# Moving the further block to the seventh pair, w3 of the last pair in three loads, and another order of the last sums and of the last norm

## The chip, the core and the metric

The kernel runs on one core of a Trainium2 chip. The metric is the device time of one execution in microseconds; the median of three runs of the kernel before is 714.94 us (714.26 to 716.94). A core has five engines that run side by side and meet only at semaphores: TensorE (PE in the rows; PEld is its weight load), VectorE (DVE), ScalarE (ACT), GpSimd (POOL) and SyncE (SP), which here issues nearly all DMA transfers.

## What is computed

One layer of an encoder: 512 tokens of width 1024 go through a mixer and then through a mixture of 32 experts with a normed output. The mixer takes the first third of the time and is not touched. Cut to the part that the change touches, the reference is:

```python
# h: the normed tokens (512 x 1024); two experts are chosen for each token
hid = jax.nn.silu(xb @ w1[e]) * (xb @ w3[e])      # w1, w3: 1024 x 512, for each expert e
y   = (hid @ w2[e]) * wt[:, None]                 # w2: 512 x 1024
out = out.at[row_tok].add(y)                      # back to the tokens
x   = x + g2 * out
return rms_norm(x) * final_g
```

All is float32. The weights of the 32 experts are 192 MB, read once.

## The kernel before

**Pairs.** The experts are worked through two at a time, in 16 pairs (`pair(p)`, p = 0 to 15; the last is `LAST`). Each expert has 64 places for tokens (`CAP`), so a pair fills the 128 partitions. For a pair TensorE multiplies with w1 (`up_product(n0, xg, 0)`, line L1002), then adds up four groups of the pair before (`combine_before`, L1024 and L1025: two products for each of the eight groups of 128 tokens by 512 columns), multiplies with w3 (L1002 again), adds up the other four groups, turns the hidden rows (L971), turns the rows gathered for the next pair (L963), and multiplies with w2 in two halves of 512 columns (`down_half`, L1016). VectorE weighs each half with the router's weight (`weighted`, L1895), ScalarE makes its high part (L1514), VectorE its low part (`low_part`, L1900); these feed the sums of the next pair. VectorE adds each finished group to the tokens (L1905).

**Weights.** The six matrices of a pair are six units of 2 MB. Unit n goes to slot n modulo 9 (eight slots of `ring` and one of `mid`). SyncE loads the units in order (`expert_unit`, L518) and waits before each for the slot to be used up (`slot_used_up`), so one held slot holds back every load behind it. The loads of the last pair are cut in pieces (`last_pair_units`, L570): w1 and w3 in halves, w2 as its first 512 columns and two quarters of the others; `up_product` and `down_half` wait for the pieces one by one.

**The further block.** An expert with more than 64 tokens needs further blocks of 64; here there is one. The expert of the first of them is swapped to place `XPLACE` = 2 `XPAIR`, so that its weights come with pair `XPAIR`, and the block is worked beside that pair: its slots are made in pair `XBEGIN` = `XPAIR` - 3, its rows are turned in `XTURN` = `XPAIR` - 1 (L1033), its products run in `XPAIR` (L1046 with w1 and w3, L1061 with w2), and its sums in the two pairs behind (L1071). The three units that it uses (`HELD`) are free only after L1046 or L1061. Behind pair `LATER` = `XPAIR` + 2 every engine asks whether there are more blocks. `XPAIR` is 9.

**The end.** Behind the last w2 product TensorE adds up the eight groups of the last pair, first the four of the low 512 columns (`HALVES_FIRST`), then the four others. VectorE adds them (`last_add`). ScalarE squares each group into a sum (L1550) and takes the root for each of the four token tiles (L1565); VectorE takes the reciprocal (L2077) and scales the high half of each tile (L2079). GpSimd multiplies the low halves with `final_g` (L2167, into `gained`), and ScalarE scales them (L1555). SyncE stores a tile when both its halves are done (L602).

## Time and profile before

| | us |
|---|---|
| median of 3 runs | 714.94 (714.26 to 716.94) |
| the profiled execution, its own time | 715.57 |
| its span, first to last instruction | 712.8 |
| TensorE busy | 672.9 (94%) |
| VectorE / ScalarE / GpSimd busy | 344.5 / 177.5 / 61.6 |
| bytes moved by DMA | 253.19 MB |
| mean granted TensorE clock | 0.992 |

All times in rows are microseconds from the start of the span, unless marked ns. A row of the timeline gives start, duration, engine, line, operation and tile; "x32" means that 32 like instructions were merged. In brackets stands how long the engine was idle before, and who released it. The chain is the work that ended last, followed back from the last instruction.

### The profile page before, as it was taken

The page shows a single profiled execution, that of the slowest core. Times are in us where ns is not written, and L with a number is a line of the kernel's source. Part 1 is how long each engine was busy: PE and PEld are TensorE (multiplying, and loading weights), DVE is VectorE, ACT ScalarE, POOL GpSimd, SP SyncE. Part 2 cuts the span into 40 slices and gives each one's busy share as a digit, 9 for nine tenths or more (in the row PEclk, how much of TensorE's full clock was granted, in tenths as well). Part 3 has the DMA queues.
Part 4 walks back from the last instruction along what each step waited for, and adds up shares of the span by engine and source line. Part 5 has one row for each costly group of instructions (what it writes and reads, how often), then busy time and mean ns, then how long its engine had stood idle before and what let it go on. Part 6 is the DMA issues. An engine that isn't in the chain of part 4 may idle for free.

```text
span 712.8 us, 9269 instructions
## 1 busy us (share of the span) xinstructions
PE 672.9 (94%) x3703; PEld 364.6 (51%) x3703; DVE 344.5 (48%) x648; ACT 177.5 (25%) x322; POOL 61.6 (9%) x59
## 2 busy tenths in 40 slices
PE   2999999999999899999999998898999999999993
PEld 2676787866878434344344343443344343443441
DVE  3546988798977723333334332332144433332336
ACT  4333468323424211110110110101021110111115
POOL 2017900100000100000000000000000000000003
PEclk9999999999999999999999999999999999999997
DMA  9998355666369599999999999999999999999982
GB/s 330 388 375 315 118 189 195 241 235 235 117 238 354 226 419 431 424 425 428 426 425 427 427 427 424 417 425 426 428 426 428 426 425 428 425 425 425 417 332 118
DMA packets 41595, 253.19 MB, mean 355 GB/s; under 512 B 4304, under 2 KB 4688, under 8 KB 28496
## 3 DMA queue, kind: packets, MB, share of 16 engines
q1 hardware_dynamic: 37008, 243.82, 83.8%
q0 software_dynamic: 2624, 4.74, 1.8%
q10 hardware_dynamic: 1920, 4.04, 1.5%
q8 instruction: 30, 0.49, 0.3%
q14 instruction: 13, 0.11, 0.0%
HBM read 252.84 MB, written 4.19 MB: 361 GB/s over the span
## 4 chain that ended last, share of the span: by engine, by line
PE 78%; DMA 15%; ACT 3%; DVE 3%; issue 1%; ACTq 0%; SPq 0%; POOLq 0%; DVEq 0%
PE bank L1002 26%; PE bank L692 18%; DMA ring<-in_w 13%; PE bank L1016 13%; PE bank L1024 3%; PE bank L1025 3%; PE bank L963 2%; PE bank L639 1%; PE bank L816 1%; PE bank L1046 1%; PE bank L971 1%; PE bank L656 1%; PE bank L794 1%; PE bank L804 1%; DMA xg_rows<-x_rows,keep 1%
## 5 line engine op out<-in xcount | busy, mean ns | idle before, releaser
L1002 PE MATMUL bank<-ring,low 128*64 128x512 f32 x944 | 228.8, 598 | 9.9 <-DMA ring<-in_w 8.7
L1002 PEld LDWEIGHTS bank<-ring,low 128*64 128x64 f32 x944 | 75.2, 138 | 130.3 <-issue 129.4
L1905 DVE TENSOR_TENSOR x<-x,bank 128x512 f32<-128x512 f32 x136 | 84.5, 681 | 80.9 <-PE bank L1025 80.9
L1016 PE MATMUL bank<-ring,low 128*64 128x512 f32 x432 | 114.0, 596 | 0.3 <-ACT low L1502 0.3
L1016 PEld LDWEIGHTS bank<-ring,low 128*64 128x64 f32 x432 | 35.0, 137 | 64.8 <-issue 63.0
L1895 DVE SCALAR_TENSOR_TENSOR y_raw<-bank,keep,g2b 128x512 f32<-128x512 f32 x32 | 24.0, 750 | 86.7 <-PE bank L1016 86.7
L2021 DVE TENSOR_TENSOR low<-low,bank 128x512 f32<-128x512 f32 x16 | 11.0, 688 | 97.8 <-PE bank L1002 97.8
L1024 PE MATMUL bank<-y_hi,slot_tok 128*128 128x512 f32 x128 | 53.7, 419 | 0.2 <-DVE y_lo L1900 0.2
L1502 ACT COPY low<-bank 128x512 f32<-128x512 f32 x16 | 9.4, 586 | 165.7 <-PE bank L971 165.7
L1025 PE MATMUL bank<-y_lo,slot_tok 128*128 128x512 f32 x128 | 50.4, 393 | 0.0
L2133 POOL DMA_INDIRECT xg_rows<-x_rows,keep x16 | 16.0, 999 | 372.7 <-PE bank L963 288.4
L1514 ACT CAST y_hi<-y_raw 128x512 fp32r<-128x512 f32 x32 | 19.8, 618 | 106.5 <-DVE y_raw L1895 106.5
L692 PE MATMUL bank<-h_hi,w_hi 128*128 128x512 f32 x96 | 38.4, 400 | 1.1 <-DVE h_lo L1614 1.1
L1024 PEld LDWEIGHTS bank<-y_hi,slot_tok 128*128 128x128 f32 x128 | 24.0, 187 | 29.1 <-issue 24.3
L692 PE MATMUL bank<-h_lo,w_hi 128*128 128x512 f32 x96 | 37.4, 390 | 0.0
L692 PE MATMUL bank<-h_hi,w_lo 128*128 128x512 f32 x96 | 37.4, 390 | 0.0
L1002 PE MATMUL bank<-mid,low 128*64 128x512 f32 x80 | 35.4, 595 | 0.7 <-DMA ring<-in_w 0.7
L1016 PE MATMUL bank<-mid,low 128*64 128x512 f32 x80 | 35.6, 596 | 0.0
L1609 DVE TENSOR_TENSOR w_lo<-ring,w_hi 128x512 fp32r<-128x512 f32 x32 | 25.0, 785 | 20.4 <-ACT w_hi L1299 20.2
L1496 ACT ACTIVATE low<-bank 128x512 f32<-128x512 f32 x16 | 9.6, 599 | 99.6 <-PE bank L1002 99.6
L1900 DVE TENSOR_TENSOR y_lo<-y_raw,y_hi 128x512 fp32r<-128x512 f32 x32 | 22.1, 692 | 21.3 <-ACT y_hi L1514 21.2
L1299 ACT CAST w_hi<-ring 128x512 fp32r<-128x512 f32 x32 | 19.7, 617 | 39.5 <-PE bank L692 34.2
(279 smaller groups left out, 890.2 us busy)
## 6 DMA issues: line engine op xcount, KB each, us to landing
ring<-in_w SPq DMA_DIRECT2D x76, 2048.0 KB, 27.1
ring<-in_w_mod SPq DMA_DIRECT2D x11, 2048.0 KB, 11.7
mid<-in_w SPq DMA_DIRECT2D x10, 2048.0 KB, 28.7
ring<-in_w SPq DMA_DIRECT2D x18, 1024.0 KB, 24.7
ring<-in_w_in SPq DMA_DIRECT2D x3, 2048.0 KB, 22.5
ring<-in_w_out SPq DMA_DIRECT2D x2, 2048.0 KB, 11.0
x<-in_x SPq DMA_DIRECT2D x4, 512.0 KB, 5.5
ring<-in_w_in SPq DMA_DIRECT2D x2, 1024.0 KB, 18.7
```

Of the source, the lines that this page charges most:

```text
L692: last = mm(out_, lhs, rhs, start=k == 0 and n == 0, stop=stop and n == 2)
L1002: last = mm(bk[e * CAP:(e + 1) * CAP, :], xb[:, k, e * CAP:(e + 1) * CAP], unit(n % SLOTS, KD)[:, k, :], start=k == 0, stop=k == KD - 1)
L1016: last = mm(bk[e * CAP:(e + 1) * CAP, :], hid_t[:, k, e * CAP:(e + 1) * CAP], unit(n % SLOTS, KF)[:, k, hf * 512:(hf + 1) * 512], start=k ...
L1024: mm(bk[:, :], slot_tok[:, buf, t * P:(t + 1) * P], hi[:, c], start=True, stop=False)
L1025: return mm(bk[:, :], slot_tok[:, buf, t * P:(t + 1) * P], lo[:, c], start=False, stop=True)
L1299: nc.scalar.copy(w_hi[:, c % DEPTH, :], raw_chunk(c)).then_inc(w_hi_ready, 1)
L1514: nc.scalar.copy(y_hi[:, c], y_raw[:, c]).then_inc(yh_ready, 1)
L1609: v.tensor_tensor(lo, raw_chunk(c), hi.bitcast(F32), ALU.subtract).then_inc(w_lo_ready, 1)
L1895: return v.scalar_tensor_tensor(raw[:, c], (Y0, Y1)[hf][:, :], w_slot[:, buf:buf + 1], g2b[:, c], ALU.mult, ALU.mult)
L1900: return v.tensor_tensor(lo[:, c], raw[:, c], hi[:, c].bitcast(F32), ALU.subtract)
L1905: return v.tensor_tensor(acc[:, t, c], acc[:, t, c], bk[:, :], ALU.add)
L2133: return g_.indirect_dma_start(rows_[:, :], None, x1_row, bass.IndirectOffsetOnAxis(ap=row_of[:, buf:buf + 1], axis=0), bounds_check=S - 1 ...
```

## The change

Four things are changed. `XPAIR` goes from 9 to 6, and with it the place of the swapped expert and every step of the further block. The w3 units of the last pair are loaded in three pieces (half, quarter, quarter) in place of two halves; `up_product` waits for the pieces with a new semaphore `third_in`. In the last pair the first four sums stand ahead of the last quarter of the w2 product, and with them VectorE's first four adds and ScalarE's first four squares stand ahead of the second half's low and high parts. In the last norm GpSimd scales the low halves of tiles 0 and 1, and ScalarE those of tiles 2 and 3, behind all its squares and roots.

```diff
-XPAIR = 9
+XPAIR = 6
...
             def last_pair_units(k):
-                pieces = (((slice(0, kk // 2), slice(0, 512)), (slice(kk // 2, kk), slice(0, 512))) if k < 4 else
-                          ((slice(0, kk), slice(0, 512)), (slice(0, kk // 2), slice(512, D)),
-                           (slice(kk // 2, kk), slice(512, D))))
+                pieces = (((slice(0, 4), slice(0, 512)), (slice(4, KD), slice(0, 512))),
+                          ((slice(0, 4), slice(0, 512)), (slice(4, 6), slice(0, 512)), (slice(6, KD), slice(0, 512))),
+                          ((slice(0, KF), slice(0, 512)), (slice(0, 2), slice(512, D)), (slice(2, KF), slice(512, D))))[k // 2]
+                second_in = third_in if k < 4 else middle_in
...
-                sp.wait_ge(fin_low, t + 1)
+                if t < 2:
+                    sp.wait_ge(fin_low_pool, t + 1)
+                else:
+                    sp.wait_ge(fin_low, t - 1)
...
-                        if k == KD // 2 and n0 == FIRST[LAST]:
-                            pe.wait_ge(landed[n % SLOTS], landed_at(n))
+                        if n0 == FIRST[LAST]:
+                            if k == 4 and w == 1:
+                                pe.wait_ge(third_in[e], 16)
+                            elif k == (4, 6)[w]:
+                                pe.wait_ge(landed[n % SLOTS], landed_at(n))
...
+            def last_sums(hf):
+                pe.wait_ge(yl_ready, 2 * LAST + 1 + hf)
+                for i in range(4 * hf, 4 * hf + 4):
+                    combine_group(HALVES_FIRST[i], LAST % BUFS, y_hi, y_lo, EXTRA_BANKS[i]).then_inc(c_done, 1)
...
+                if p == LAST:
+                    down_half(n0, 0).then_inc(y_done, 1)
+                    down_half(n0, 1, 0, KF // 2)
+                    pe.wait_ge(pt_ready, PAIRS)
+                    pe.wait_ge(acc_done, 8 * LAST)
+                    last_sums(0)
+                    down_half(n0, 1, KF // 2, KF).then_inc(y_done, 1)
+                    last_sums(1)
+                    return
...
             for t in range(NT):
                 halfs_square(t, 1, ssq)
                 act.wait_ge(fin_ssq, NT + t + 1)
                 a(rstd[:, t:t + 1], ssq[:, t:t + 1], ACT.Sqrt, bias=norm_bias[:, t:t + 1], scale=1.0 / D).then_inc(fin_std, 1)
-                if t > 0:
-                    low_half_scaled(t - 1)
-            low_half_scaled(NT - 1)
+            for t in range(2, NT):
+                low_half_scaled(t)
...
+            for t in range(2):
+                pool.wait_ge(fin_rec, t + 1)
+                pool.wait_ge(fin_gain, t + 1)
+                g_.tensor_scalar(acc[:, t, 0:512], gained[:, t, :], rstd[:, t:t + 1], None, ALU.mult).then_inc(fin_low_pool, 1)
```

TensorE's program at the end of the last pair, before (bank3 and bank4 hold the two halves of the w2 product, `last_pair_middle_in` and `landed4`, `landed5` tell of the two quarters of the second half):

```order
L1016 MATMUL bank3<-ring_49,low_52 64x512 x7
L1016 MATMUL bank4<-ring_49,low_52 64x512 [waits last_pair_middle_in0]
L1016 MATMUL bank4<-ring_49,low_52 64x512 [waits landed4]
L1016 MATMUL bank4<-ring_49,low_52 64x512 [waits landed5]
L1024 MATMUL bank2<-y_hi_68,slot_tok_80 128x512 [waits acc_done,yl_ready,sil_ready,pt_ready]
L1024 MATMUL bank5<-y_hi_68,slot_tok_80 128x512 [waits yl_ready]
```

The same place after (L1024 is now the w2 product, L1032 the first product of a sum):

```order
L1024 MATMUL bank3<-ring_49,low_52 64x512 x7
L1024 MATMUL bank4<-ring_49,low_52 64x512 [waits last_pair_middle_in0]
L1032 MATMUL bank2<-y_hi_68,slot_tok_80 128x512 [waits yl_ready,acc_done,pt_ready]
L1024 MATMUL bank4<-ring_49,low_52 64x512 [waits landed4]
L1024 MATMUL bank4<-ring_49,low_52 64x512 [waits landed5]
L1032 MATMUL bank5<-y_hi_68,slot_tok_80 128x512 [waits yl_ready]
```

The first sums, with their wait for the low part of the first half (`yl_ready`), have moved from behind the last quarter of the w2 product to ahead of it.

ScalarE's program in the last norm, before (from the root of tile 0 on; `ring_49` is where `gained` lies):

```order
L1565 ACTIVATE keep_54<-keep_54,ring_49 128x1 [waits fin_ssq]
L1550 ACTIVATE xg_rows_79,keep_54<-x1_50 128x512 [waits acc_done]
L1565 ACTIVATE keep_54<-keep_54,ring_49 128x1 [waits fin_ssq]
L1555 ACTIVATE x1_50<-ring_49,keep_54 128x512 [waits fin_gain,fin_rec]
L1550 ACTIVATE more_unread_82,keep_54<-x1_50 128x512 [waits acc_done]
```

And after:

```order
L1543 ACTIVATE xg_rows_79,keep_54<-x1_50 128x512 [waits acc_done]
L1580 ACTIVATE keep_54<-keep_54,ring_49 128x1 [waits fin_ssq]
L1543 ACTIVATE more_unread_82,keep_54<-x1_50 128x512 [waits acc_done]
L1580 ACTIVATE keep_54<-keep_54,ring_49 128x1 [waits fin_ssq]
L1572 ACTIVATE x1_50<-ring_49,keep_54 128x512 [waits fin_gain,fin_rec] x2
```

The scalings no longer stand between the squares and roots; two are left, at the end.

## Rows read from the trace of the kernel before

**Rows 1.** The page, 40 equal slices of the span: GB/s that the DMA engines moved.

```profile
GB/s 330 388 375 315 118 189 195 241 235 235 117 238 354 226 419 431 424 425 428 426 425 427 427 427 424 417 425 426 428 426 428 426 425 428 425 425 425 417 332 118
```

**Rows 2.** Waits of TensorE, 240 to 698 us: total, times, longest.

```profile
PE bank L1002 <- DMA ring<-in_w: 9.4, 6, 3.1
```

**Rows 3.** The chain that ended last, from 640 us on: start, us, what.

```profile
624.86 29.14 DMA ring<-in_w
...
654.14 7.09 PE bank L1002 x32
...
680.66 7.02 PE bank L1002 x32
...
690.50 7.10 PE bank L1016 x32
...
697.63 0.76 DVE y_raw L1895
...
699.07 0.69 DVE y_lo L1900
```

**Rows 4.** Line L570, issue at 683.2 us, the last piece of w2: issue, landing.

```profile
L570 SPq DMA_DIRECT2D ring<-in_w x1: 1106/1106/1106, 683.2 to 683.2; - x1
DMA to landing us min/median/max: 11.0/11.0/11.0
```

**Rows 5.** Line L518, last load ahead of the held slots, pair 9: issue, landing.

```profile
L518 SPq DMA_DIRECT2D mid<-in_w x1: 376/376/376, 489.7 to 489.7; - x1
DMA to landing us min/median/max: 36.6/36.6/36.6
```

**Rows 6.** Line L518, the same load three pairs earlier: issue, landing.

```profile
L518 SPq DMA_DIRECT2D mid<-in_w x1: 377/377/377, 400.5 to 400.5; - x1
DMA to landing us min/median/max: 34.9/34.9/34.9
```

**Rows 7.** Timeline of TensorE, 400 to 600 us: two products of pair 9.

```profile
492.20 8.78 PE L1002 MATMUL bank<-ring,low 128*64 128x512 f32 x32 [3.08 <-DMA ring<-in_w]
...
509.87 7.04 PE L1046 MATMUL bank<-ring,low 128*64 128x512 f32 x32
```

**Rows 8.** Timeline of VectorE, last pair: low part of the first half, an add.

```profile
695.63 0.69 DVE L1900 TENSOR_TENSOR y_lo<-y_raw,y_hi 128x512 fp32r<-128x512 f32 x1 [0.68 <-ACT y_hi L1514]
...
698.30 0.68 DVE L1905 TENSOR_TENSOR x<-x,bank 128x512 f32<-128x512 f32 x1
```

**Rows 9.** Timeline of TensorE, last pair: first and last product of four sums.

```profile
697.52 0.50 PE L1024 MATMUL bank<-y_hi,slot_tok 128*128 128x512 f32 x1
...
699.24 0.39 PE L1025 MATMUL bank<-y_lo,slot_tok 128*128 128x512 f32 x1
```

**Rows 10.** Timeline of ScalarE, last norm: square, root, next square, last two scalings.

```profile
702.71 0.63 ACT L1550 ACTIVATE xg_rows<-x 128x512 f32<-128x512 f32 x1
...
703.46 0.29 ACT L1565 ACTIVATE keep<-keep,ring 128x1 f32<-128x1 f32 x1
703.66 0.61 ACT L1550 ACTIVATE xg_rows<-x 128x512 f32<-128x512 f32 x1
...
707.71 1.32 ACT L1555 ACTIVATE x<-ring,keep 128x512 f32<-128x512 f32 x2
```

**Rows 11.** Timeline of GpSimd, mixer: scaling of one tensor, then products of two.

```profile
65.91 1.50 POOL L2116 TENSOR_SCALAR ring<-ring 128x512 f32<-128x512 f32 x1
...
69.12 3.95 POOL L2110 TENSOR_TENSOR ring<-ring 128x518 f32<-128x518 f32 x3
```

**Rows 12.** Timeline of VectorE, mixer: one operation beside each of these.

```profile
66.53 0.69 DVE L1609 TENSOR_TENSOR w_lo<-ring,w_hi 128x512 fp32r<-128x512 f32 x1 [0.76 <-ACT w_hi L1299]
...
72.09 1.52 DVE L1609 TENSOR_TENSOR w_lo<-ring,w_hi 128x512 fp32r<-128x512 f32 x1
```

**Rows 13.** Timeline of GpSimd, last norm: the four products into gained.

```profile
699.12 5.51 POOL L2167 TENSOR_TENSOR ring<-x,ring 128x512 f32<-128x512 f32 x4 [59.40 <-DVE x L1905]
```

**Rows 14.** Line L2079, VectorE's four scalings: min, median, max ns.

```profile
L2079 DVE SCALAR_TENSOR_TENSOR x<-x,keep,ring x4: 750/752/1128, 704.1 to 708.0; 128x512 f32<-128x512 f32 x4
```

More of the change, by code:

```diff
@@ L383, in build @@
         middle_in = [sem(f"last_pair_middle_in{e}") for e in range(2)]
+        third_in = [sem(f"last_pair_w3_third_quarter_in{e}") for e in range(2)]
         a_done, sil_ready, hid_ready, t_done, hidt_ready = sems(
@@ L391, in build @@
             "extra_transposed extra_hidt extra_down extra_yf extra_yh extra_yl extra_combined extra_added lists_chain")
[L392 to L393 removed]
+        fin_table, tail_in, fin_ssq, fin_std, fin_rec, fin, fin_low, fin_low_pool, fin_gain, fin_bias, stored = sems(
+            "fin_table tail_in fin_ssq fin_std fin_rec fin fin_low fin_low_pool fin_gain fin_bias stored")
         block = ctx.enter_context(nc.Block())
@@ L568, in last_pair_units @@
                         src = w[:, bass.ds(experts_of(LAST)[e], 1), r, c].rearrange("p e k n -> p (e k) n")
-                        done = landed[n % SLOTS] if i == len(pieces) - 1 else (begun[k + e], middle_in[e])[i]
+                        done = landed[n % SLOTS] if i == len(pieces) - 1 else (begun[k + e], second_in[e])[i]
                         sp.dma_start(unit(n % SLOTS, kk)[:, r, c], src).then_inc(done, 16)
@@ L1004, in up_product, with down_half @@
                 return last
-            def down_half(n0, hf):
+            def down_half(n0, hf, k0=0, k1=KF):
                 bk = (Y0, Y1)[hf]
-                for k in range(KF):
+                for k in range(k0, k1):
                     for e in range(2):
@@ L1234, in _ @@
                     further_rounds(pe, another_block, another_begin)
-            pe.wait_ge(pt_ready, PAIRS)
-            pe.wait_ge(sil_ready, PAIRS)
-            pe.wait_ge(acc_done, 8 * LAST)
-            for i, g in enumerate(HALVES_FIRST):
-                if i % 4 == 0:
-                    pe.wait_ge(yl_ready, 2 * PAIRS - 1 + i // 4)
-                combine_group(g, (PAIRS - 1) % BUFS, y_hi, y_lo, EXTRA_BANKS[i]).then_inc(c_done, 1)
         def part_free(eng, c):
@@ L1516, in pair, with halfs_square @@
                         extra_begin(0)
+                    if p == LAST and hf == 0:
+                        act.wait_ge(fin_table, 1)
+                        for t in range(NT):
+                            halfs_square(t, 0, first_ssq)
                 if p == XPAIR:
                     extra_high_part(0)
+            def halfs_square(t, hf, sums):
+                act.wait_ge(acc_done, 8 * LAST + HALVES_FIRST.index(2 * t + hf) + 1)
+                c = slice(hf * 512, (hf + 1) * 512)
+                unread = xg_rows[:, t * 512:(t + 1) * 512] if t < 2 else more_unread[:, t - 2, :]
+                a(unread, acc[:, t, c], ACT.Square, accum_out=sums[:, t:t + 1]).then_inc(fin_ssq, 1)
             def extra_silu(j):
@@ L1542, in _ @@
                     further_rounds(act, another_block, extra_begin)
-            act.wait_ge(fin_table, 1)
-            def halfs_square(t, hf, sums):
-                act.wait_ge(acc_done, 8 * LAST + HALVES_FIRST.index(2 * t + hf) + 1)
-                c = slice(hf * 512, (hf + 1) * 512)
-                unread = xg_rows[:, t * 512:(t + 1) * 512] if t < 2 else more_unread[:, t - 2, :]
-                a(unread, acc[:, t, c], ACT.Square, accum_out=sums[:, t:t + 1]).then_inc(fin_ssq, 1)
             def low_half_scaled(t):
@@ L1555, in low_half_scaled @@
                 a(acc[:, t, 0:512], gained[:, t, :], ACT.Copy, scale=rstd[:, t:t + 1]).then_inc(fin_low, 1)
-            for t in range(NT):
-                halfs_square(t, 0, first_ssq)
             act.wait_ge(fin_ssq, NT)
@@ L2032, in pair @@
                     weighted(y_raw, p % BUFS, hf).then_inc(yf_ready, 1)
-                    if p == LAST and hf == 1:
-                        last_add(HALVES_FIRST[0])
                     dve.wait_ge(yh_ready, 2 * p + 1 + hf)
                     low_part(y_lo, y_raw, y_hi, hf).then_inc(yl_ready, 1)
+                    if p == LAST:
+                        for i in range(4):
+                            last_add(HALVES_FIRST[4 * hf + i])
                     if p == XBEGIN and hf == 0:
@@ L2070, in _ @@
                     further_rounds(dve, another_block, extra_begin)
-            for g in HALVES_FIRST[1:]:
-                last_add(g)
             dve.wait_ge(tail_in, 16)
```

2 lines of the change are left out of this document (removed).

## The prediction

> **What bounds the kernel now.** I read four views in this order. First the page's 40 slices: from the fifteenth slice on the DMA engines move 417 to 431 GB/s, slice after slice, and leave off only in the last three [rows 1]. The transfer of the weights therefore sets the pace of most of the run. Then the waits of TensorE in that part: it stands for weights 6 times, 9.4 us in all [rows 2], so its own work is nearly as long as the stream, and the two alternate as the bound. Then the chain that ended last [rows 3]: its last transfer lands at 654.0 (624.86 + 29.14), TensorE begins the w3 product of pair 14 at 654.14, and from there to the end the chain runs through engines. What stands ahead of 654 can reach the end only by moving that landing. Last the timelines of the final 20 us on TensorE, VectorE and ScalarE [rows 8 to 10]: one chain of single instructions from the last w2 product to the last scaling, which ends at 709.03 (707.71 + 1.32); the last store and the end of the span lie 3.8 us behind.
>
> The sum is made against the profiled execution, 715.57 us, whose span is 712.8. It lies 0.63 above the median of 714.94, which I take off at the end.
>
> **1. The further block, from pair 9 to pair 6.** Nothing is added or removed: the same products run and the same bytes move. TensorE gets its extra products three pairs earlier, so it falls behind the stream earlier and has no time to wait in pairs 6 to 9; the stream, which does not care, gains on it there and loses the lead again, at the same rate, behind pair 9. The 9.4 us of waits [rows 2] should then appear in later pairs, 11 to 14, and the landing at 654.0 [rows 3] should stand. Price: 0. The bound below: before, one slice, the 26th (446 to 463 us), moves 417 GB/s beside neighbours of 424 and 425 [rows 1]; it lies ahead of the held slots' time (490 to 517), where the slices are full. If that dip comes from the order of work around it and the new order has none, the stream comes earlier by 8/425 of a slice of 17.8 us, 0.3 us.
>
> What could go wrong is a hole in the new place. SyncE's load behind the held slots waits until the extra product is done. In pair 9 that product ends at 516.91 (509.87 + 7.04) [rows 7], while the last load ahead, issued at 489.7, lands at 526.3 [rows 5]: 9.4 us to spare. The same load of pair 6 is issued at 400.5 and lands at 435.4 [rows 6]. If the extra product ends as long after that issue as in pair 9 (516.9 - 489.7 = 27.2), it ends at 427.7, 7.7 us ahead of the landing. So the queue does not run dry, and the price stays 0; each microsecond beyond those 7.7 would be one microsecond at the end.
>
> **2. w3 of the last pair in three pieces.** One more load and one more wait for each expert. The w3 product of the last pair ran 7.02 us, as long as products that stand behind nothing [rows 3, 7], so none of its waits had anything to wait for; with a smaller last piece they have still less. The further load costs SyncE one issue, which for the last piece took 1.1 us, 11.0 us ahead of its landing [rows 4]; the stream is queued that deep, which hides it. The last piece of w2 lands at 694.2 and TensorE wants it only at 695.75 (below), so 1.5 us cover what a further split costs the transfer. Price: 0.
>
> **3. First sums ahead of the last quarter of w2.** This lengthens the path to the second half of the product. TensorE begins w2 at 690.50 and takes 7.0 us for 16 steps [rows 3]; 12 of them (eight of the first half, four of the second) end at 690.50 + 12/16 x 7.0 = 695.75. There it now waits for the low part of the first half, which VectorE ends at 695.63 + 0.69 = 696.32 [rows 8]; with 0.06 for the signal it goes on at 696.38, a wait of 0.63. Then come the eight products of four sums: 697.52 to 699.24, and 0.23 (their spacing) for the last [rows 9], 1.95 us. The remaining quarter follows, and behind it in TensorE's queue everything else. VectorE's weighting of the second half (y_raw) begins not at 697.63 [rows 3] but 0.63 + 1.95 later: **+2.57**, at 700.20.
>
> What that buys comes behind it. Before, from 697.63 to the first square of the second four groups, 702.71 [rows 10], there were 5.08 us, in which VectorE did all four adds of the first groups too. Now these adds are done, and what is left is: start of y_raw to end of y_lo 2.13 (697.63 to 699.07 + 0.69) [rows 3]; 0.06 to the first sum; 0.78 from a sum's start to its add (697.52 to 698.30) [rows 8, 9]; the add 0.68; 0.09 to ScalarE. That is 3.74: **-1.34**. The first of the last four squares begins at 703.94.
>
> **4. Two scalings from ScalarE to GpSimd.** Before, from the first of the last squares to the end of the last scaling: 702.71 to 709.03, 6.32 us [rows 10]. Now ScalarE does four squares with their roots and then two scalings: 0.95 for each square and root (702.71 to 703.66), three times, 0.75 to the fourth root, 0.20 for it, and 1.32 for two scalings: 5.12, **-1.20**, ending at 709.06. GpSimd must be ready by then. A scaling of one tensor took it 1.50 [rows 11]; its four products into gained took 5.51 [rows 13] and can start behind the first add, which is at about 697.2 (sum at 696.38 + 0.78) and ends at 697.84, so they end near 703.4. The reciprocal of tile 0 is there at about 705.2 (703.94 + 0.95 + 0.3), the two scalings end near 708.2: 0.8 ahead of ScalarE.
>
> The sum of 3 and 4 is +2.57 - 1.34 - 1.20 = +0.03.
>
> **5. VectorE beside GpSimd.** What is new is that the second half's low part (near 701.6, two operands in SBUF) falls beside GpSimd's products, and VectorE's scalings beside GpSimd's. In the mixer a like operation of VectorE took 1.52 beside GpSimd's products of two tensors, and 0.69 beside its scaling of one [rows 11, 12]. So the low part costs 0 to +0.83. Of VectorE's four scalings the one that stood beside GpSimd's product took 1128 ns, the others 750 [rows 14]: +0.38 for each that meets one, and only the last is on the path, with 0.2 of slack. I take +0.4 for all of it, the middle, and keep 0 to +1.2 as bounds.
>
> The Trainium skill, "SBUF — State Buffer", section "Who interferes with whom", states that a VectorE instruction with two SBUF inputs contends with a GpSimd instruction that reads SBUF, and that the shared port pair is held for a whole instruction. The row of 1.52 agrees with the first; the 0.69 begun at 66.53, inside the scaling of 65.91 to 67.41, does not show a hold for the whole instruction. By the page alone the forecast would be that of the second rival.
>
> Forecast: 715.57 + 0.03 + 0.4 = 716.0 for the profiled execution, less 0.63: **715.4**. Its own range, with the bounds of 1 and 5: 714.7 to 716.2.
>
> **The rivals.** *The stream comes earlier.* If the landing at 654.0 comes earlier, TensorE's last two pairs move with it. For it speaks the 26th slice [rows 1], worth 0.3; against it, all others up to the last three are full. With nothing lost in 5 as well, 715.57 + 0.03 - 0.3 to -1.2 - 0.63: 713.8 to 714.7.
>
> *GpSimd holds VectorE for whole instructions (the slower side).* Place: the last norm. If VectorE's instruction cannot begin until GpSimd's ends, the low part waits up to 1.38 (5.51/4) [rows 13], and the scalings of tiles 1 and 2 wait up to 1.3 each, with the reciprocals behind them that ScalarE's scalings need: +4.0 in place of +0.4, 719.0. It decides from the point where VectorE's instruction starts second. Against it speak the 0.69 of [rows 12] and the three 750s of [rows 14].
>
> *A slow product behind a late wait.* Behind the longest wait, 3.08 us, the product took 8.78 and not 7.09 [rows 3, 7], 1.69 more. There, in pair 9, the slack to the stream took it up. With the waits moved towards the end, one of that length at pair 14 or 15 would have nothing behind it to take it up: 715.4 + 1.7 = 717.1. For it: the waits do move there; against: only one wait of 6 had that effect.
>
> *The stream runs dry at the held slots.* The 7.7 us of part 1 are too few, because TensorE or SyncE is later in pair 6 than in pair 9: 716 to 720, one for one.
>
> **How the numbers follow.** Half a per cent, 3.6 us, is about what a measurement of this kernel can tell from no change: 711.4 to 718.5. Chances: forecast 0.60; earlier stream 0.15; slow product 0.10; GpSimd holds VectorE 0.08; stream dry 0.07, half of it over 718.5. Slower is 0.08 + 0.035, rounded down to 0.10 since the holds need not all meet; faster would need a gain no part shows, 0.03; same 0.87. The range from 713.7 to 717.6 holds the first three (0.85) and ends where the last two begin.
>
> **What would show it.** Right: TensorE's waits for weights sit in pairs 11 to 14 and again add up to about 9; the w3 product of pair 14 begins at 654.1; the last quarter of w2 stands behind a wait of 0.6 and four sums, y_raw of the second half near 700.2; the first of the last squares near 703.9; the last scaling ends between 709 and 710; the w3 product of the last pair has no inner wait. Wrong: slices under 420 GB/s near 420 to 440 us; a start other than 654.1 in pair 14; a low part or scalings of VectorE that start 1 us or more behind what releases them; a last chain that ends on GpSimd.

## The result, and the profile after

The changed kernel takes 719.72 us (median of 4 runs, 718.28 to 720.45) beside 714.78 for the kernel before in the same measurement: a ratio of 1.0065, 95% interval 1.0048 to 1.0082. A second measurement gave 720.17 and 1.0076 (1.0061 to 1.0091). I had forecast 715.4, in a range of 713.7 to 717.6, and had given "slower by over 0.5%" one chance in ten. The profiled execution took 720.45 us, its span is 718.5.

**The stretch up to the last pair.** The page's 40 slices of the kernel after (GB/s moved):

```profile
GB/s 331 388 375 304 117 201 180 250 221 234 118 246 340 267 421 429 429 423 429 422 414 422 429 429 423 428 426 422 431 423 426 429 426 426 424 429 421 406 222 117
```

TensorE's waits from 240 us on in the same profile (total, times, longest):

```profile
PE bank L1010 <- DMA ring<-in_w: 11.5, 8, 3.4
PE bank L1032 <- DVE y_lo L1914: 3.8, 2, 3.2
```

The stream is as full as before [rows 1]; at 413 to 449 us, where the held slots now are, it moves 429 and 423. The waits for weights are 11.5 us in place of 9.4 [rows 2]. The second row is new: TensorE waits for the low part of the last pair, 3.2 us at one time. The timeline of TensorE, from pair 14 on (start, duration, engine, line, operation, tiles, count, idle time before it and its releaser):

```profile
645.08 7.09 PE L1010 MATMUL bank<-ring,low 128*64 128x512 f32 x32 [3.42 <-DMA ring<-in_w]
654.88 7.09 PE L1010 MATMUL bank<-ring,low 128*64 128x512 f32 x32 [0.66 <-DMA ring<-in_w]
691.25 5.37 PE L1024 MATMUL bank<-ring,low 128*64 128x512 f32 x24 [0.30 <-ACT low L1517]
697.22 0.47 PE L1032 MATMUL bank<-y_hi,slot_tok 128*128 128x512 f32 x1 [0.60 <-DVE y_lo L1914]
699.23 1.94 PE L1024 MATMUL bank<-ring,low 128*64 128x512 f32 x8
704.37 0.50 PE L1032 MATMUL bank<-y_hi,slot_tok 128*128 128x512 f32 x1 [3.20 <-DVE y_lo L1914]
```

The w3 product of pair 14 begins at 654.88, 0.74 later than before [rows 3], right behind the landing of its weights; so the last w2 product begins at 691.25 and not at 690.50. From there to the end of the span there were 22.3 us before (690.50 to 712.8); now there are 27.25 (691.25 to 718.5). **The tail is 4.95 us longer**: of the 5.70 by which the two profiled spans differ, all but the 0.75 that stand ahead of it.

**The tail.** VectorE, then ScalarE, then GpSimd, in the timeline after:

```profile
701.22 0.75 DVE L1909 SCALAR_TENSOR_TENSOR y_raw<-bank,keep,g2b 128x512 f32<-128x512 f32 x1 [0.79 <-PE bank L1024]
702.66 1.66 DVE L1914 TENSOR_TENSOR y_lo<-y_raw,y_hi 128x512 fp32r<-128x512 f32 x1 [0.69 <-ACT y_hi L1529]
705.26 0.69 DVE L1919 TENSOR_TENSOR x<-x,bank 128x512 f32<-128x512 f32 x1 [0.94 <-PE bank L1033]
707.82 0.69 DVE L1919 TENSOR_TENSOR x<-x,bank 128x512 f32<-128x512 f32 x1 [0.17 <-PE bank L1033]
708.42 0.16 DVE L2090 RECIPROCAL keep<-keep 128x1 f32<-128x1 f32 x1
710.39 0.15 DVE L2090 RECIPROCAL keep<-keep 128x1 f32<-128x1 f32 x1
```

```profile
706.04 0.63 ACT L1543 ACTIVATE xg_rows<-x 128x512 f32<-128x512 f32 x1 [3.22 <-DVE x L1919]
706.80 0.29 ACT L1580 ACTIVATE keep<-keep,ring 128x1 f32<-128x1 f32 x1
710.57 1.58 ACT L1572 ACTIVATE x<-ring,keep 128x512 f32<-128x512 f32 x2 [0.66 <-DVE keep L2090]
```

```profile
698.79 4.97 POOL L2180 TENSOR_TENSOR ring<-x,ring 128x512 f32<-128x512 f32 x4 [62.33 <-DVE x L1919]
708.68 4.07 POOL L2184 TENSOR_SCALAR x<-ring,keep 128x512 f32<-128x512 f32 x2 [4.92 <-DVE keep L2090]
```

Four things are to be seen. The low part at 702.66 lies inside GpSimd's four products and takes 1.66, where the first half's took 0.69 [rows 8]; it ends at 704.32, 0.56 behind the end of these products (703.76). Tile 0's root is done at 707.09 (706.80 + 0.29), but its reciprocal begins at 708.42, behind the fourth add. GpSimd's two scalings wait for that and take 4.07, not 3.0 (1.50 apiece in [rows 11]). ScalarE waits 0.66 for a reciprocal, and is done at 712.15; GpSimd is done last, at 712.75.

The granted clock of TensorE there (columns: stretch, its length, busy time of PE, PEld, DVE, ACT, POOL with counts, granted clock as a share of full speed, DMA share, GB/s):

```profile
701.00:704.00 3.00, 0.17 (x2) 0.00 (x0) 2.10 (x2) 1.11 (x4) 2.77 (x3) 1.00 0.00 0
704.00:705.00 1.00, 0.63 (x2) 0.49 (x3) 0.32 (x1) 0.00 (x0) 0.00 (x0) 0.93 0.00 0
705.00:706.00 1.00, 1.00 (x4) 0.78 (x3) 0.69 (x1) 0.00 (x0) 0.00 (x0) 0.50 0.00 0
```

TensorE is idle for 3.20 us, and soon behind that the clock is at its lower level (0.50, 1.2 GHz) for the second sums. Their adds come 0.85 apart (705.26 to 707.82, three intervals); two products at full clock, 0.23 apart [rows 9], would let them come as fast as VectorE adds, 0.68 or less [rows 8].

**The stores.** GB/s in 40 slices of 700 to 722 us, first of the kernel before, then of the kernel after:

```profile
GB/s 0 0 0 0 0 0 0 0 0 0 0 290 402 261 365 424 216 402 410 395 395 253 0 0 0 0 30 0 0 0 0 0 0 0 0 0 0 0 0 0
```

```profile
GB/s 0 0 0 0 0 0 0 0 0 0 0 0 0 0 0 0 0 0 0 0 0 283 410 261 89 387 417 402 402 387 432 343 0 0 0 0 0 0 0 0
```

The line of the stores in the profile after (issue durations in ns, first and last start, then issue to landing in us), and the landings of the kernel before under it:

```profile
L607 SPq DMA_DIRECT2D out<-x x4: 337/374/731, 710.9 to 713.7; - x4
...
DMA to landing us min/median/max: 2.6/3.1/4.3
```

```profile
DMA to landing us min/median/max: 2.6/2.6/3.3
```

Before, the stores start as tiles come out and two slices of 261 and 216 stand between them; they have the rate nearly to themselves. After, three of them leave in one block without a gap, since SyncE issues them in the order of the tiles and the second waits for GpSimd's second scaling. Behind the last scaling there were 3.8 us to the end of the span (709.03 to 712.8); now there are 5.75 (712.75 to 718.5).

### The profile page after: what moved, and what is told of

It is laid out like the page before. It is cut to its first block, busy times and chain, and to the rows that moved or that the text cites. A ratio compares the mean times of both kernels' runs of the same rounds, so it can differ in the third digit from the quotient of the medians.

```text
span 718.5 us, 9274 instructions
## 1 busy us (share of the span) xinstructions
PE 673.3 (94%) x3703; PEld 366.0 (51%) x3703; DVE 346.1 (48%) x648; ACT 176.2 (25%) x320; POOL 65.1 (9%) x61
## 4 chain that ended last, share of the span: by engine, by line
PE 73%; DMA 18%; DVE 3%; ACT 2%; issue 2%; POOL 1%; POOLq 0%; SPq 0%; DVEq 0%
PE bank L1010 24%; PE bank L697 18%; DMA ring<-in_w 17%; PE bank L1024 11%; PE bank L1032 3%; PE bank L1033 3%; PE bank L968 2%; PE bank L644 1%; PE bank L821 1%; PE bank L1054 1%; PE bank L976 1%; PE bank L661 1%; PE bank L799 1%; PE bank L657 1%; PE bank L809 1%
## 5 line engine op out<-in xcount | busy, mean ns | idle before, releaser
L1010 PE MATMUL bank<-ring,low 128*64 128x512 f32 x944 | 227.8, 598 | 11.5 <-DMA ring<-in_w 10.8
L1024 PE MATMUL bank<-ring,low 128*64 128x512 f32 x432 | 114.2, 596 | 0.3 <-ACT low L1517 0.3
L1024 PEld LDWEIGHTS bank<-ring,low 128*64 128x64 f32 x432 | 34.8, 137 | 64.7 <-issue 63.0
L1032 PE MATMUL bank<-y_hi,slot_tok 128*128 128x512 f32 x128 | 54.3, 424 | 3.8 <-DVE y_lo L1914 3.8
L1032 PEld LDWEIGHTS bank<-y_hi,slot_tok 128*128 128x128 f32 x128 | 24.3, 190 | 33.3 <-issue 25.0
L1024 PE MATMUL bank<-mid,low 128*64 128x512 f32 x80 | 35.6, 596 | 0.0
```

Of the source, the lines that this page charges most:

```text
L1010: last = mm(bk[e * CAP:(e + 1) * CAP, :], xb[:, k, e * CAP:(e + 1) * CAP], unit(n % SLOTS, KD)[:, k, :], start=k == 0, stop=k == KD - 1)
L1024: last = mm(bk[e * CAP:(e + 1) * CAP, :], hid_t[:, k, e * CAP:(e + 1) * CAP], unit(n % SLOTS, KF)[:, k, hf * 512:(hf + 1) * 512], start=k ...
L1032: mm(bk[:, :], slot_tok[:, buf, t * P:(t + 1) * P], hi[:, c], start=True, stop=False)
```

## The experiments

Each is the changed kernel with parts put back or added. Two measures: the time, with its ratio to the kernel before on the same chip, and the **tail** of the profiled execution, from the start of the last w2 product to the end of the span. The tail leaves out the scatter of the weights' stream; the spans are given to 0.1 us, so a tail is good to 0.05. Not all kernels were measured on one chip, so small differences between two medians of the table are weak; the kernel before had 714.58 to 714.89 in the five measurements.

| kernel | median us | ratio (95% interval) | tail us |
|---|---|---|---|
| before | 714.6 to 714.9 | 1 | 22.30 |
| changed kernel, first and second measurement | 719.72, 720.17 | 1.0065 (1.0048, 1.0082), 1.0076 (1.0061, 1.0091) | 27.25, 27.28 |
| w3_alone | 714.40 | 0.9998 (0.9986, 1.0009) | 22.28 |
| block_alone | 716.16 | 1.0014 (1.0003, 1.0024) | 22.36 |
| block_alone_again | 715.39 | 1.0009 (0.9998, 1.0020) | 22.30 |
| block_filled | 715.00 | 1.0007 (0.9997, 1.0016) | 22.37 |
| block_filled_again | 715.22 | 1.0005 (0.9997, 1.0014) | 22.31 |
| sums_alone | 717.51 | 1.0039 (1.0025, 1.0053) | 24.77 |
| gained_held | 716.27 | 1.0026 (1.0016, 1.0036) | 24.80 |
| scaling_alone | 716.41 | 1.0020 (1.0007, 1.0034) | 23.75 |
| scaling_uncontended | 715.51 | 1.0009 (0.9998, 1.0020) | 23.00 |
| stores_reordered | 715.33 | 1.0013 (1.0002, 1.0024) | 23.19 |
| scaling_split_stores | 715.23 | 1.0008 (0.9997, 1.0018) | 23.33 |
| split_stores | 714.66 | 0.9998 (0.9988, 1.0008) | 22.01 |
| sums_and_scaling | 718.87 | 1.0056 (1.0042, 1.0070) | 26.40 |
| sums_filled | 718.09 | 1.0055 (1.0039, 1.0070) | 26.39 |
| after_mended | 718.16 | 1.0051 (1.0035, 1.0067) | 25.75 |

### One part at a time

**w3_alone**: the kernel before with the third piece of w3.

> The kernel before with w3 of the last pair in three pieces and nothing else. Theory (no product waits inside w3 there, before or after; the split costs at most what the later landing of w2's last quarter has to spare): 714.6, the kernel before's, within 0.4; no wait of TensorE inside the last w3 product, the last quarter of w2 landing before it is asked for. Rival (the further descriptors delay the stream's end or SyncE): 0.5 or more slower, with a wait in the w2 product.

Measured 714.40, a ratio of 0.9998; the tail 22.28. It costs nothing, as forecast.

**block_alone**: the kernel before with

```diff
-XPAIR = 9
+XPAIR = 6
```

> The kernel before with the further block in pair 6 and nothing else. Theory (all the loss is at the end of the kernel, and the later landing of the profile after is scatter of the stream): TensorE's waits move to pairs 11 to 14, its w3 product of pair 14 begins at 654.0 plus or minus 0.7, the time is that of the kernel before, 714.8, within 0.7. Rival (the move delays the stream): the w3 product of pair 14 begins at 654.9 as in the profile after, and the time is 715.5 or more.

Measured 716.16. The tail is untouched; what is longer lies ahead of it. The timeline of TensorE in pair 14, and then the granted clock there (columns as above):

```profile
644.58 10.00 PE L1005 MATMUL bank<-ring,low 128*64 128x512 f32 x32 [3.21 <-DMA ring<-in_w]
656.55 7.09 PE L1005 MATMUL bank<-ring,low 128*64 128x512 f32 x32
```

```profile
645.00:650.00 5.00, 5.00 (x14) 1.62 (x12) 0.00 (x0) 0.00 (x0) 0.00 (x0) 0.50 1.01 429
```

The long wait now stands in pair 14; behind it w1 ran at 0.50 and took 10.00 us, so w3 began at 656.55, 2.15 behind the landing of its weights (654.40), and nothing later takes that up. It is the third of my rivals, in this execution. Neither expectation named it.

**sums_alone**: the kernel before with the first sums ahead of the last quarter (core of the edit):

```diff
-                    down_half(n0, 1).then_inc(y_done, 1)
-                    last_sums(0)
+                    down_half(n0, 1, 0, KF // 2)
+                    last_sums(0)
+                    down_half(n0, 1, KF // 2, KF).then_inc(y_done, 1)
                     last_sums(1)
```

> The kernel before with the first four sums ahead of the last w2 quarter and nothing else. Theory: the second half's y_raw begins 2.7 to 2.9 later than before, its low part takes 1.5 to 1.7 beside GpSimd's products, the second four sums run at half the clock after an idle time of some 3 us (spacing 0.43, not 0.23), VectorE's first reciprocal stands behind the fourth add, and ScalarE, which has the scaling of tile 0 between its squares, waits for it: the last scaling ends 3 to 4 us later than in the kernel before, 718 us. Rival (the order of the sums is even by itself, as I had predicted, 2.57 lost and 1.34 plus what ScalarE gains won back): 715.5 to 716.5.

Measured 717.51, the tail 2.47 longer: nearer to the theory's 718 than to the rival, but not the theory in all its parts; the last scaling ends 2.48 later and not 3 to 4. The low part took 1.67, the reciprocal stood behind the fourth add; the clock, though, stayed at 1.00 in this execution (sums 0.23 apart) although TensorE had been idle for the same 3.20 us.

**scaling_alone**: the kernel before with GpSimd's two scalings (and ScalarE's two at the end).

> The kernel before with the low halves of tiles 0 and 1 scaled by GpSimd and nothing else. Theory (GpSimd's scalings take 2.0 and the stores stand in SyncE's queue in the order of the tiles, so that the last three go out together and land 1.3 us apart): GpSimd's second scaling ends near 708.5, ScalarE's last one near 707.9, the store of tile 3 lands 4.3 us and not 3.3 behind its issue, and the time is 715.5 to 716.5, slower by 1 us although ScalarE is done 1.1 us earlier. Rival (ScalarE's chain is the end, as I had predicted): its 1.2 us appear in the time, 713.6.

Measured 716.41, the tail 1.45 longer, though the last scaling ends earlier. ScalarE's and GpSimd's last scalings in its timeline, and then the landings of the four stores:

```profile
705.53 1.49 ACT L1566 ACTIVATE x<-ring,keep 128x512 f32<-128x512 f32 x2
...
703.67 3.95 POOL L2182 TENSOR_SCALAR x<-ring,keep 128x512 f32<-128x512 f32 x2
```

```profile
DMA to landing us min/median/max: 2.6/3.1/4.3
```

From the start of w2 (689.55) GpSimd is done 18.07 later, at 707.62, ScalarE 17.47 later; before, the last scaling ended 18.53 behind that start. So 0.46 is gained in the scalings and 1.9 lost in the stores behind them: the theory.

**sums_and_scaling**: both, without the move of the block and the third piece.

> The changed kernel with the further block back in pair 9 and w3 of the last pair in two pieces. Theory (all of the loss is in these two parts): 718.5 to 719.7, the time of the changed kernel. Rival (the move of the block or the third piece takes a part): 0.7 or more below the changed kernel's time, 719.0 or less.

Measured 718.87; the tail is 4.10 longer, 2.47 + 1.45 and a little. The rival's "0.7 or more below" is met as well (719.72 or 720.17 less 718.87 is 0.85 to 1.3). This need not be the block's move alone: in the profiles the tails differ by 0.85 too (27.25 and 26.40), and that is TensorE's clock in these executions (see sums_filled). The medians do not separate the two.

### What the block's move costs

**block_filled** and **block_filled_again** (block_alone with idle products ahead of the wait), beside **block_alone_again**:

```diff
+                if p == LAST - 1:
+                    unread(11, A1)
                 weights(0)
```

> block_alone with 11 idle products of 128 columns (results unread) on TensorE ahead of its wait for the first weights of pair 14, where it stood idle for 3.2 us in block_alone's profile; they take some 2.5 us. Theory (the move costs because the long wait now stands in pair 14, the clock falls to 0.50 behind it in part of the executions, and nothing behind takes up the lost 1.3 to 2.9 us): the w1 product of pair 14 takes 7.1 us in the profile, the w3 product begins right behind its landing, and the median falls from 716.2 to about 715.0. Rival (the move delays the stream itself by about a microsecond): the median stays at 716 and the landing of pair 14's w3 is at 654.5 or later.

> block_alone once more, beside block_filled's kernel on the same chip. Theory (the loss is the fallen clock behind the long wait of pair 14, in part of the executions): 0.8 to 1.5 above block_filled_again; where the profile shows no slow product in pair 14, the profiled execution's time is within 0.7 of the kernel before's. Rival (the difference of the two came from the chips): equal within 0.4.

> block_filled once more, beside block_alone's kernel on the same chip. Theory: 0 to 0.5 above the kernel before, w1 of pair 14 in 7.1 us. Rival (chips): as block_alone_again.

In the profile of block_filled the idle products run, and w1 keeps its 7.09:

```profile
641.28 1.42 PE L654 MATMUL bank<-keep 128*128 128x128 f32 x11
644.11 7.09 PE L1005 MATMUL bank<-ring,low 128*64 128x512 f32 x32 [1.41 <-DMA ring<-in_w]
```

In block_alone_again w1 of pair 14 took 8.78 behind a wait of 2.88, and w3 began 0.93 behind its landing (654.01 against 653.08). So the mechanism is there in two of two profiles without the idle products and in none of two with them. Its size is not shown: on one chip the medians differed by 0.17 (the rival's "equal within 0.4"), over both pairs of measurements by 0.5 (715.64 of 23 runs, 715.14 of 24), but the first pair came from two chips. The execution of block_alone_again with the slow product took 714.84, the least of its twelve, and block_filled_again lies 0.62 above the kernel before, a little more than expected. And the slow product is not all: the changed kernel's own two profiles have w1 of pair 14 at 7.09 and still begin the last w2 product at 691.25 and 691.42.

**after_again** is the changed kernel once more.

> The changed kernel once more, with its profile. Theory (low part beside GpSimd's products 0.97, the second sums at the fallen clock up to 0.83, reciprocals behind the fourth add, GpSimd's scalings 2.0 apiece, stores in a bunch): 718.3 to 720.5, 27.0 plus or minus 0.4 from the start of the last w2 product to the end of the span (22.3 in the kernel before), whatever the landing of pair 14's w3, which scatters by 0.8 to either side. Rival (the landing of 654.74 is the change's own): it lands again at 654.6 or later.

The tail is 27.28, the theory; the landing is 654.93, the rival. Over all profiles the landing of pair 14's w3 lies at 653.05 to 654.48 with the block in pair 9 (eleven profiles, mean 653.8) and at 653.08 to 654.93 with it in pair 6 (seven, mean 654.2): the ranges overlap. The start of the last w2 product has the means 690.3 and 691.1. The move of the block thus seems to cost about 0.8 us ahead of the tail (0.42 to 1.45 by the medians of block_alone and block_filled, of whose four intervals three take in a ratio of 1). In block_alone's profile the slow product is the cause; what it is in the changed kernel, a later stream or its scatter, stays open.

### What the tail is made of

**gained_held**: sums_alone with GpSimd's products held back.

```diff
             pool.wait_ge(tail_in, 16)
+            pool.wait_ge(yl_ready, 2 * PAIRS)
             for t in range(NT):
```

> sums_alone with GpSimd's four products into gained held back until the second half's low part is done. Theory (VectorE's low part takes 1.67 and not 0.69 because it falls beside these products): it takes 0.69, TensorE's idle time falls from 3.2 to 2.2, and the time falls by 1.0 from 717.5 to 716.5. Rival (VectorE's wait for its turn at the operands is not what sets the end, ScalarE's scalings wait for the products now): 717.5 or more.

VectorE and TensorE in its timeline:

```profile
701.91 0.69 DVE L1910 TENSOR_TENSOR y_lo<-y_raw,y_hi 128x512 fp32r<-128x512 f32 x1 [0.68 <-ACT y_hi L1524]
706.40 1.89 DVE L2088 SCALAR_TENSOR_TENSOR x<-x,keep,ring 128x512 f32<-128x512 f32 x1
...
702.66 0.50 PE L1027 MATMUL bank<-y_hi,slot_tok 128*128 128x512 f32 x1 [2.23 <-DVE y_lo L1910]
```

The low part takes 0.69 again: GpSimd's products made it 1.67. The median fell by 1.24. In the profiled execution (717.09, above the median) the tail is not shorter, 24.80: there VectorE's first scaling met the products instead and took 1.89, and the clock fell in the second sums. Held back, the contention moves on by one step, and wins only in part.

How VectorE loses this time can be read too. First two lines of VectorE at the end of the kernel before (the last seven adds, the first scaling), then a scaling of GpSimd in its mixer with VectorE's operation inside it, then GpSimd's products in gained_held:

```profile
699.68 4.26 DVE L1905 TENSOR_TENSOR x<-x,bank 128x512 f32<-128x512 f32 x7
704.05 1.13 DVE L2079 SCALAR_TENSOR_TENSOR x<-x,keep,ring 128x512 f32<-128x512 f32 x1
```

```profile
74.42 1.49 POOL L2116 TENSOR_SCALAR ring<-ring 128x512 f32<-128x512 f32 x1
74.75 0.84 DVE L1609 TENSOR_TENSOR w_lo<-ring,w_hi 128x512 fp32r<-128x512 f32 x1 [0.46 <-ACT w_hi L1299]
```

```profile
702.74 4.99 POOL L2177 TENSOR_TENSOR ring<-x,ring 128x512 f32<-128x512 f32 x4 [64.03 <-DVE y_lo L1910]
```

VectorE's operation with two operands in SBUF ends about 0.55 behind the end of GpSimd's products, however long it takes: 704.32 against 703.76 in the kernel after (1.66), 705.18 against 704.63 before (1.13, [rows 13]), 73.61 against 73.07 in the mixer (1.52, [rows 11, 12]), 708.29 against 707.73 in gained_held (1.89, through the end of the third and the whole fourth product). In the tails of the 18 profiles there are 17 such operations, and all of them end 0.54 to 0.56 behind the product. So VectorE waits until the product has ended; it does not run beside it at a lower speed. Beside a scaling of one tensor the wait is shorter: there the operation ends 0.32 ahead of GpSimd's (75.59 against 75.91).

**sums_filled**: sums_and_scaling with twelve idle products between the last w2 quarter and the second sums.

```diff
                     down_half(n0, 1, KF // 2, KF).then_inc(y_done, 1)
+                    for _ in range(12):
+                        mm(Y0[:, :], slot_tok[:, LAST % BUFS, 0:P], y_hi[:, 0:512], start=True, stop=True)
                     last_sums(1)
```

> sums_and_scaling with 12 idle products of 512 columns (results unread) on TensorE between the last w2 quarter and the second four sums, where it stood idle for 3.2 us. Theory (the idle time lets the clock fall to 0.50, the second sums then space at 0.43 and VectorE's reciprocals stand behind their adds): the sums space at 0.23 at a granted clock of 1.00, the first reciprocal comes up to 0.8 earlier, and the median is 0.3 to 0.8 below sums_and_scaling's 718.9. Rival (the clock does not matter, since ScalarE's squares and roots at 0.95 a tile set the pace): within 0.2 of 718.9.

The idle products in TensorE's timeline, and then the stretch 704 to 705 with its clock (columns as above):

```profile
699.66 3.01 PE L1216 MATMUL bank<-y_hi,slot_tok 128*128 128x512 f32 x12
702.99 0.50 PE L1030 MATMUL bank<-y_hi,slot_tok 128*128 128x512 f32 x1 [0.32 <-DVE y_lo L1914]
```

```profile
704.00:705.00 1.00, 1.00 (x5) 0.56 (x3) 1.00 (x3) 0.45 (x1) 0.00 (x0) 1.00 0.00 0
```

The clock holds. The median is 0.78 lower, at the edge of what was expected, but from another chip, and the tail is the same, 26.39 and 26.40: in the profile of sums_and_scaling the clock fell only near the end of the second sums (0.89 in 704 to 705), and cost nothing. Where it falls at once, as in the changed kernel's two profiles, the first reciprocal begins 17.17 and 17.24 behind the start of w2, and not 16.34: **0.83 to 0.90**.

**scaling_uncontended**: scaling_alone without VectorE's four scalings.

> scaling_alone with VectorE's four scalings of the high halves left out (the reciprocals stay, the high halves are stored unscaled). Theory (GpSimd's scalings take 2.0 and not the mixer's 1.5 because VectorE's scalings, with two operands in SBUF, run beside them): 1.5 apiece, the second ends 0.8 to 1.0 earlier, and the time is 1.0 or more below scaling_alone's 716.4. Rival (GpSimd's scaling takes 2.0 here for a reason of its own, such as the scale from a column or the rows it writes): 2.0 apiece again, and 716.0 or more.

```profile
703.81 3.12 POOL L2179 TENSOR_SCALAR x<-ring,keep 128x512 f32<-128x512 f32 x2
```

GpSimd's two scalings take 3.12 in place of 3.95: it is VectorE's company that makes them slow. (The median is 0.9 lower, a little under the expected 1.0.) In scaling_alone each of the two begins while a scaling of VectorE has 0.56 and 0.52 left to run, and takes 0.44 and 0.40 more than the 1.56 of scaling_uncontended, 0.12 less than what was left, both times: so GpSimd waits for the rest of VectorE's operation. VectorE's scalings pay too: the second and the fourth, begun in the midst of one of GpSimd's, take 0.99, and 0.75 alone.

**stores_reordered**: scaling_alone with the stores in another order.

```diff
-            for t in range(NT):
+            for t in (0, 2, 3, 1):
                 sp.wait_ge(fin, t + 1)
```

> scaling_alone with SyncE's stores in the order of tiles 0, 2, 3, 1, so that no store stands behind the wait for GpSimd's second scaling. Theory (the three last stores go out together and land 1.3 apart, so the end is set by when they may start and not by the last scaling alone): tiles 2 and 3 go out near 706.4 and 707.4 on scaling_alone's scale, the last store lands 0.6 earlier, and the median falls by 0.5 to 0.8, from 716.4 to 715.8. Rival (the end is the last scaling, GpSimd's second one, plus a fixed time): the order changes nothing, 716.4.

Measured 715.33, 1.08 below scaling_alone, the tail 0.56 shorter, with GpSimd's scalings as long as there (3.95). The order in SyncE's queue was a cost by itself, though only about a third of the 1.9: the four stores still go out within 2.0 us (3.7 in the kernel before) and land 1.3 apart.

**scaling_split_stores** and **split_stores**: each tile's high and low half stored apart, on scaling_alone and on the kernel before.

```diff
                 sp.wait_ge(fin, t + 1)
+                sp.dma_start(out_r[:, t, 512:D], acc[:, t, 512:D]).then_inc(stored, 16)
                 sp.wait_ge(fin_low, t + 1)
-                sp.dma_start(out_r[:, t, :], acc[:, t, :]).then_inc(stored, 16)
+                sp.dma_start(out_r[:, t, 0:512], acc[:, t, 0:512]).then_inc(stored, 16)
```

> scaling_alone with the stores split in the same way. Theory (stores stand behind GpSimd's scalings in SyncE's queue and leave together): the high halves of tiles 0 and 1 no longer wait, the last landing comes 0.6 to 1.0 earlier than scaling_alone's, 715.4 to 715.8, still above the kernel before. Rival (nothing but the last scaling's end counts): 716.4.

> The kernel before with each tile's high half and low half stored apart, as soon as each is done. Theory (the end of the kernel is the last store, 2.0 to 2.6 us of fixed time and 1.3 us for 512 KB, behind the queue of the others): the last one is half as long, the last landing comes 0.5 to 0.7 earlier, 714.0. Rival (the fixed time of eight issues on SyncE eats it, or the rate of the stores as a whole is the bound): 714.4 or more.

(The lines are those of split_stores; on scaling_alone the wait in the middle is that of the changed kernel.) On scaling_alone the split wins back 0.42 of the tail, less than expected, and 1.2 in the median. On the kernel before it shortens the tail by 0.29, which the time doesn't show (714.66, the rival; ratio 0.9998): the only version with a shorter tail than the kernel before, and not a measurable gain.

**after_mended**: the changed kernel with both sets of idle products and the stores in the order 0, 2, 3, 1.

> The changed kernel with three mendings at once: 11 idle products ahead of pair 14's first weights, 12 between the last w2 quarter and the second sums, and the stores in the order 0, 2, 3, 1. Theory (each of the three mechanisms is there in the changed kernel and they add up): 719.7 less 1.1, 0.8 and 0.7 to 1.1, which is 716.7 to 717.1; what is left over the kernel before, some 2.2, is the second half's delay with the contended low part. Rival (they cover one another, the slowest one alone sets the end): 718 or more.

Measured 718.16, the rival's "718 or more", 1.6 to 2.0 below the changed kernel and not 2.6 to 3.0; the tail 25.75, shorter by 1.50. That is 0.83 of the clock and 0.65 of the stores, and it leaves 0.1 to 0.5 of the medians for the mending in pair 14. (In its profile the last w2 product begins at 690.15, 1.1 earlier than in the changed kernel's first, but one profile of each does not tell this from the scatter of the landing.)

## Why the prediction was wrong

**Part 1, the block: nearly right.** The stream didn't run dry: the extra product ended at 424.99 (417.92 + 7.07) and the slices at 413 to 449 us are full. The waits went to pairs 11 to 14. But the price of 0 seems too low by about 0.8. In block_alone it came from the place that I had named for a rival, a long wait in pair 14 with a slow product behind it; in the changed kernel's two profiles that product was not slow, and where its 0.7 to 0.9 (691.25 and 691.42 against 690.50) come from stays open.

**Part 2, w3: right**, 0.9998.

**Part 3, the sums: the first terms right, what came behind them wrong.** I had y_raw 2.57 later; by the tail's scale it was 2.84 later (701.22 - 691.25 against 697.63 - 690.50). The wait of 0.60 for the first half's low part and the four sums are there as worked out. The failing step is the "-1.34" for the way from y_raw to the first of the last squares: I took the low part at its uncontended length, and it measured 4.82 (701.22 to 706.04) and not 3.74, so that only 0.26 of the 5.08 came back.

**Part 5, VectorE beside GpSimd: the right place, the wrong size.** The low part's row of 1.52 was the bound, and 0.4 was taken for everything as "the middle". But by my own times (the low part near 701.6, the products up to 703.4) the low part was certain to fall inside the four products, and then the nearest row is the contended one; it cost 0.97. And I looked at one side only: GpSimd's scalings were priced from a row of the mixer, 1.50, where VectorE's operation began behind GpSimd's; at the end each began behind a scaling of VectorE that was still running, waited for it, and took 2.03 on average.

**Part 4, the scalings: wrong in two steps that were not in the sum at all.** First, the reciprocal of tile 0: I let it follow its root, and in VectorE's program it stands behind all four adds (708.42, while the root was done at 707.09). Before, the last add and the first root ended at about the same time, 703.9 and 703.75 [rows 10]. Now that the first square begins behind the first of only four adds, the other three are still to come when the root is done, at the lower clock above all: the reciprocal began 1.33 behind the root's end, and 0.57 behind it in sums_alone, at full clock. Second, I ended the sum at the last scaling and took the 3.8 us behind it as fixed. They weren't: 5.75.

The account of the tail, on its own scale (from the start of w2; forecast 22.3 + 0.03 + 0.4, measured 27.25): y_raw later than forecast by 0.27; the low part 0.97; the first add at the lower clock 0.11; GpSimd's end later than the end that I forecast for ScalarE, 1.59 (712.75 against 706.04 + 5.12), from the late reciprocal (1.38) and the slow scalings (1.07), less the 0.86 by which GpSimd had been forecast to be done first; the stores 1.98 (5.75 against 3.77). Together 4.92, of which 0.4 had been granted: the 4.5 that are missing.

**The rivals.** "GpSimd holds VectorE for whole instructions" would have given 719.0, near the result, and in part by the right way: the low part did wait for the end of GpSimd's product, 0.97 of the "up to 1.38". The rest of its 4.0 did not come: beside GpSimd's scalings of one tensor two of VectorE's four took 0.99 in place of 0.75, and what else made the end late, GpSimd waiting for VectorE, the reciprocal behind the adds and the bunched stores, the rival did not have. I had the wait in hand and argued it away. The row of 1.52 in [rows 12] ends 0.54 behind the products of [rows 11]; the scaling of 1128 ns in [rows 14] is the line at 704.05 above, 0.55 behind the products of [rows 13]. What I set against it was no evidence: the three scalings of 750 ns ran after GpSimd's products had ended (704.63; the next scaling began at 705.29), and the 0.69 of [rows 12] began late in its scaling, where the same operation, begun earlier, took 0.84.

Of the Trainium skill's "SBUF — State Buffer", section "Who interferes with whom", the runs bear out that a VectorE instruction with two SBUF inputs contends with GpSimd's reads (gained_held, scaling_uncontended). The hold for a whole instruction agrees with the rows of GpSimd's two-tensor products (0.55 behind their end, each time) and not with those of its scalings (0.32 ahead of their end).

"A slow product behind a late wait" is seen in block_alone, not in the changed kernel's two profiles. The range was too narrow because its upper end came from one of these at a time; the costs stand one behind another in a single chain and add up.

## What to carry to other kernels

Work handed to an idle engine at the end of a kernel is priced on both engines that share operands there, with the wait of each for what the other has begun, and up to the last landing: the stores belong to the chain, and an in-order queue passes on the latest of them. Where the order of sums is changed, read in each engine's program what now stands between a result and the next that needs it (here four adds ahead of a reciprocal). And measure a tail from a fixed event in the same profile, here the start of the last product: it repeats within 0.1 us (22.28 to 22.37 in the five profiles of changed kernels that leave the tail as it was), where whole times scatter by 2.

## What was not expected of the hardware

Behind 3.2 us of idle time TensorE's clock fell to 0.50 early in the second sums in two profiles of the changed kernel, only near their end in sums_and_scaling, and not at all within them in sums_alone, with the same idle time in each; in gained_held it fell within them behind 2.2 us. Behind waits of 1.9 to 3.4 us for weights it was the same: products of 8.78 and 10.00 us in some executions, 7.09 in others. Idle products in the gap kept it at 1.00 behind it in each of the four profiles that had them. Of two engines that contend for operands in SBUF the one that began second waited: VectorE's operation ended 0.55 behind a GpSimd product of two tensors, whatever its own length became (1.12 to 1.89 at the ends), and GpSimd's scaling grew from 1.56 to 2.0 behind a scaling of VectorE, where VectorE's own, begun inside GpSimd's, grew only from 0.75 to 0.99.
